# Expert stages of a mixture-of-experts trunk in fp32 blocks of 64 tokens on two column halves of TensorE

## The reference

```python
def moe(h, w_router, router_bias, w1, w3, w2):        # 16 experts, top 2 of one group
    idx, gate = route(ht, w_router, router_bias)       # T tokens -> 2 experts each
    ...                                                # slots sorted by expert, in blocks
    def expert_block(args):
        e, tok, g = args
        xb = ht[tok]                                   # rows gathered, 1024 wide
        hid = jax.nn.silu(xb @ w1[e]) * (xb @ w3[e])   # 1024 -> 512, twice
        return (hid @ w2[e]) * g[:, None]              # 512 -> 1024
    ...                                                # each token: sum of its two rows
```

## Time and profile before

| | us |
|---|---|
| three timed runs | 1637.46, 1641.4, 1643.38, median 1641.4 |
| the profiled execution | 1641.54, its span 1639.8 |
| PE busy over the span | 1403.7 (86%) |
| DVE busy | 1111.4 (68%) |
| ACT busy | 714.6 (44%) |
| bytes moved by DMA | 357.57 MB |

### The profile page before, as it was taken

How to read it: one execution, slowest core, us unless ns; L and a number is a source line. 1 busy time by engine, 2 the same in 40 slices (tenths; PEclk the granted TensorE clock), 3 DMA queues, 4 the chain that set the end, 5 groups by cost and what they waited for, 6 DMA issues and landing times. The chain is left out here.

```text
span 1639.8 us, 20695 instructions
## 1 busy us (share of the span) xinstructions
PE 1403.7 (86%) x6750; PEld 985.6 (60%) x6751; DVE 1111.4 (68%) x1475; ACT 714.6 (44%) x822; POOL 163.1 (10%) x144
## 2 busy tenths in 40 slices
PE   4788989457967899999999299799996789999990
PEld 2454555224446788888887144388653678878770
DVE  2379999974777886596553451376556788888844
ACT  3101101042345685585552330166433567777732
POOL 0000000000321010011010200000002101112201
PEclk9899999778988999999999599899997899999995
DMA  9457456308017997799564600040161799999935
GB/s 342 150 194 250 152 206 230 115 22 326 39 39 282 356 399 268 274 400 398 207 256 165 265 1 0 21 83 2 25 245 39 281 365 399 398 399 397 399 137 192
DMA packets 164095, 357.57 MB, mean 218 GB/s; under 512 B 7776, under 2 KB 35152, under 8 KB 164048
## 3 DMA queue, kind: packets, MB, share of 16 engines
q1 hardware_dynamic: 148848, 301.39, 50.3%
q0 software_dynamic: 8784, 31.99, 5.1%
q10 hardware_dynamic: 6416, 23.60, 3.6%
HBM read 318.57 MB, written 38.37 MB: 218 GB/s over the span
## 5 line engine op out<-in xcount | busy, mean ns | idle before, releaser
L717 DVE TENSOR_TENSOR W_LO<-W_RAW,W_HI 128x2048 fp32r<-128x2048 f32 x192 | 433.5, 2287 | 136.4 <-ACT W_HI L710 129.1
L710 ACT ACTIVATE W_HI<-W_RAW 128x2048 fp32r<-128x2048 f32 x192 | 363.0, 1912 | 97.8 <-DMA W_RAW<-in_moe_w 54.7
L1406 PE MATMUL PS<-W_HI,XLO 128*128 128x512 f32 x624 | 252.8, 405 | 28.3 <-DVE XLO L1541 28.2
L1408 PE MATMUL PS<-W_HI,XHI 128*128 128x512 f32 x624 | 247.7, 397 | 0.0
L1407 PE MATMUL PS<-W_LO,XHI 128*128 128x512 f32 x624 | 247.6, 397 | 0.0
L1184 PE MATMUL PS<-HT,RING 128*128 128x512 f32 (+1 forms) x512 | 174.6, 497 | 8.5 <-DVEq L1255 8.5
L1406 PEld LDWEIGHTS PS<-W_HI,XLO 128*128 128x128 f32 x624 | 120.0, 192 | 57.8 <-issue 25.9
L1184 PEld LDWEIGHTS PS<-HT,RING 128*128 128x128 f32 x512 | 97.6, 195 | 88.4 <-issue 72.7
L1408 PEld LDWEIGHTS PS<-W_HI,XHI 128*128 128x128 f32 x624 | 120.0, 192 | 26.2
L1407 PEld LDWEIGHTS PS<-W_LO,XHI 128*128 128x128 f32 x624 | 120.0, 192 | 23.7
L1406 PE MATMUL PS<-W_HI,HLO 128*128 128x512 f32 x312 | 124.8, 400 | 3.4 <-ACT YO L1497 3.4
(11 more groups left out here) (238 smaller groups left out, 1809.7 us busy)
## 6 DMA issues: line engine op xcount, KB each, us to landing
W_RAW<-in_moe_w SPq DMA_DIRECT2D x192, 1024.0 KB, 11.0
RING<-in_w_mod SPq DMA_DIRECT2D x24, 2048.0 KB, 14.3
moe_out<-YO ACTq DMA_DIRECT2D x39, 512.0 KB, 6.2
moe_out<-HT SPq DMA_DIRECT2D x20, 512.0 KB, 8.4
RING<-in_conv_pw SPq DMA_DIRECT2D x16, 512.0 KB, 5.3
ROWS<-rows_of_layer SPq DMA_DIRECT2D x12, 512.0 KB, 6.4
RING<-in_attn_w_qkv SPq DMA_DIRECT2D x3, 2048.0 KB, 8.1
moe_in<-RING SPq DMA_DIRECT2D x10, 512.0 KB, 3.0
```

What stands on the lines that cost most here:

```text
L710: nc.scalar.activation(part(W_HI[q], p), part(WRAW[q], p), ACT.Copy).then_inc((w2_hi if q == 2 else w_hi)[L], 1)
L717: nc.vector.tensor_tensor(part(W_LO[q], p), part(WRAW[q], p), part(W_HI[q], p).bitcast(F32), ALU.subtract).then_inc(lo[L], 1)
L1406: pe.matmul(to, lo, W_HI[q][:, at:at + 512], start=start, stop=False)
L1408: return pe.matmul(to, hi, W_HI[q][:, at:at + 512], start=False, stop=stop)
```

## The change

- A block is now 64 rows (`SUB`). `MAXB`, the index tables, the result tensor's rows and the router's arithmetic follow; INFO has a third row that tells in which of two places an expert's weights land (`home_of`).
- The products are plain fp32: no high and low parts, no `split_hi` and `split_lo`. In `up` the w3 product goes to output partitions 0 to 63 and the w1 product to 64 to 127 of one PSUM bank, by `tile_position`, each with the same 64 stationary columns; in `down` the two halves of the 1024 output columns do the same.
- Weights land in two places by the parity of the expert, and ACT (w1 and the first half of w2) and DVE (w3 and the second half of w2) copy them to the fixed place from which PE multiplies (`place`). The first expert's weights land there directly. A load waits for the same weight of the expert before to have landed and for the one before that to be copied away. Loads start after the first gather.
- Other buffers take the freed room: the combine's gathers and the QKV weight use other slots, and the QKV weight's third part is loaded before the last stores are waited for.

The diff of the stage, cut to its core (indentation reduced; `blocks_of`, `last_block`, `expert_of`, `cell_of` and `home_of` are register reads of INFO like `load_of`):

```diff
-MAXB = [TILES * 2 + NE, LT * 2 + NE]
 DEEP = [TILES, LT]
+SUB = P // 2
+DEEP_SUB = [2 * TILES, 2 * LT]
+MAXB = [2 * TILES * P // SUB + NE, 2 * LT * P // SUB + NE]
+MINB = [2 * TILES * P // SUB, 2 * LT * P // SUB]
+WSLOT = 4096
...
-    XHI = shared("XHI", [P, KT, P], F32R)
...
-    W1_HI = shared("W1_HI", [P, 4096], F32R)
-    W1_LO = shared("W1_LO", [P, 4096], F32R)
...
-    WRAW, W_HI, W_LO = (W1_RAW, W3_RAW, W2_RAW), (W1_HI, W3_HI, W2_HI), (W1_LO, W3_LO, W2_LO)
+    XT = shared("XT", [P, KT, SUB])
+    XG = shared("XG", [SUB, D])
+    YO = shared("YO", [P, 512])
+    SIL = shared("SIL", [SUB, FE])
+    HID = shared("HID", [SUB, FE])
+    HTT = shared("HTT", [P, FE // P, SUB])
+    WR = shared("WR", [P, 9 * WSLOT])
+W1, W3, W2 = (WR[:, n * WSLOT:(n + 1) * WSLOT] for n in (2, 3, 1))
...
-    return RING[:, (0, 3, 4)[q // 4], (q % 4) * D:(q % 4 + 1) * D]
-QKV_SLOT = (1, 5, 2)
+    return RING[:, (1, 2, 3)[q // 4], (q % 4) * D:(q % 4 + 1) * D]
+QKV_SLOT = (4, 0, 5)
...
+PART = WSLOT // 2
+def load_weight(sp, L, e, kind):
+    name, landed = {1: ("moe_w1", w1_in), 2: ("moe_w2", w2_in), 3: ("moe_w3", w3_in)}[kind]
+    if e:
+        for p in range(2):
+            sp.wait_ge(landed[p], e * 16)
+        at = {1: 4 + 2 * (e % 2), 3: 5 + 2 * (e % 2), 2: 8 * (e % 2)}[kind]
+    else:
+        at = {1: 2, 3: 3, 2: 1}[kind]
+    k = FE // P if kind == 2 else KT
+    src = a[name][L].rearrange("e (k p) f -> e p k f", p=P)[e]
     for p in range(2):
...
+        half = at * WSLOT + p * PART
+        sp.dma_start(WR[:, half:half + PART].rearrange("p (k f) -> p k f", k=k // 2),
+                     src[:, p * k // 2:(p + 1) * k // 2, :]).then_inc(landed[p], 16)
 def gather(pool, L):
     src = h2d[L][:, :] if L == 0 else h2d[L][0:SEQ, :]
     pool.indirect_dma_start(out=XG[:, :], out_offset=None, in_=src,
...
+                            in_offset=bass.IndirectOffsetOnAxis(ap=icur[0:SUB, 0:1], axis=0)
                             ).then_inc(xg_in[L], 16)
...
-        split_hi(act, L, 0, 0)
-        split_hi(act, L, 0, 1)
...
-            sp.wait_ge(xg_in[L], 32)
-            load_weights(sp, L, 1, (0, 1))
-            load_weights(sp, L, 0, (2,))
...
+            n = blocks_of(sp, L)
+            sp.wait_ge(xg_in[L], 16)
+            load_weight(sp, L, 0, 2)
+            for e in range(1, NE):
+                for kind, placed in ((1, (w1_placed,)), (3, (w3_placed,)),
+                                     (2, (w2_placed_low, w2_placed_high))):
+                    if e >= 3:
+                        for one in placed:
+                            sp.wait_ge(one[L], (e - 1) * (1 if kind == 2 else 2))
+                    load_weight(sp, L, e, kind)
             if L == 0:
...
+                sp.wait_ge(w3_placed[L], 2 * NE - 2)
                 load_qkv(sp, 2)
...
+                sp.wait_ge(w1_placed[L], 2 * NE - 2)
                 load_qkv(sp, 0)
-            rows = sp.compute_val(n * 16)
+                sp.wait_ge(w2_placed_low[L], NE - 1)
+                sp.wait_ge(w2_placed_high[L], NE - 1)
+                load_qkv(sp, 1)
+            rows = sp.compute_val(n * 32)
             sp.wait_ge(y_out[L], rows)
             load_row(sp, L, 1, 5, 5, gates_in[L])
             if L == 0:
                 load_row(sp, L, 0, 5, 4, gates_in[L])
-                load_qkv(sp, 1)
             else:
...
             def turn_x(b):
                 pe.wait_ge(xg_in[L], b * 16 + 16)
+                pe.sem_inc(rows_seen[L], 1)
                 for k in range(KT):
+                    ins = pe.transpose(PXT[k // 4][:, k % 4 * SUB:(k % 4 + 1) * SUB], XG[:, k * P:(k + 1) * P],
+                                       ident[0:SUB, 0:SUB])
                 ins.then_inc(xg_turned[L], 1)
...
-                pe.matmul(to, lo, W_HI[q][:, at:at + 512], start=start, stop=False)
-                pe.matmul(to, hi, W_LO[q][:, at:at + 512], start=False, stop=False)
-                return pe.matmul(to, hi, W_HI[q][:, at:at + 512], start=False, stop=stop)
-            def up(load, q, bank, done):
+            def turn_hid(b):
+                pe.wait_ge(hid_ready[L], b + 1)
+                pe.sem_inc(hid_seen[L], 1)
+                for k in range(FE // P):
+                    ins = pe.transpose(PHB[:, k * SUB:(k + 1) * SUB], HID[:, k * P:(k + 1) * P],
+                                       ident[0:SUB, 0:SUB])
+                ins.then_inc(hid_turned[L], 1)
+            def up(load, half_way):
                 for k in range(KT):
                     if k % 4 == 0:
...
+                        pe.wait_ge(w3_placed[L], load * 2 + (1 + k // 4))
+                        pe.wait_ge(w1_placed[L], load * 2 + (1 + k // 4))
+                    for g, w in enumerate((W3, W1)):
+                        ins = pe.matmul(PUV[g * SUB:(g + 1) * SUB, :], XT[:, k, :], w[:, k * FE:(k + 1) * FE],
+                                        start=(k == 0), stop=(k == KT - 1), tile_position=(0, g * SUB))
+                    if k == 3:
+                        half_way()
+                ins.then_inc(up_done[L], 1)
+            def down(load):
+                pe.wait_ge(w2_placed_low[L], load + 1)
                 for k in range(FE // P):
...
+                    if k == FE // P // 2:
+                        pe.wait_ge(w2_placed_high[L], load + 1)
+                    for c in range(2):
+                        at = k * D + c * 512
+                        ins = pe.matmul(PYO[c * SUB:(c + 1) * SUB, :], HTT[:, k, :], W2[:, at:at + 512],
+                                        start=(k == 0), stop=(k == FE // P - 1), tile_position=(0, c * SUB))
+                ins.then_inc(down_done[L], 1)
             turn_x(0)
+            for landed, placed in ((w1_in, w1_placed), (w3_in, w3_placed)):
+                for p in range(2):
+                    pe.wait_ge(landed[p], 16)
+                    pe.sem_inc(placed[L], 1)
+            pe.wait_ge(xTa[L], 1)
             pe.wait_ge(xTb[L], 1)
...
+            up(0, lambda: None)
             turn_x(1)
...
+            def block_step(b, before, y_taken):
+                load = expert_of(pe, b)
+                pe.wait_ge(xTa[L], b + 1)
                 pe.wait_ge(xTb[L], b + 1)
                 pe.wait_ge(hid_ready[L], b)
...
+                up(load, lambda: turn_hid(b - 1))
                 turn_x(b + 1)
...
+                pe.wait_ge(hT_ready[L], b)
+                if y_taken is not None:
+                    pe.wait_ge(ya_ready[L], y_taken)
+                else:
+                    for p, placed in enumerate((w2_placed_low, w2_placed_high)):
+                        pe.wait_ge(w2_in[p], 16)
+                        pe.sem_inc(placed[L], 1)
+                down(before)
+            block_step(1, 0, None)
             with pe.Fori(2, n) as b:
...
+                block_step(b, expert_of(pe, b - 1), b - 1)
+            last = last_block(pe, L)
             turn_hid(last)
...
+            pe.wait_ge(hT_ready[L], n)
+            pe.wait_ge(ya_ready[L], last)
+            down(expert_of(pe, last))
+        def place(eng, copy, L, load, home, kind, halves, placed):
+            at, landed = {1: (home + 4 * WSLOT, w1_in), 3: (home + 5 * WSLOT, w3_in), 2: (home * 4, w2_in)}[kind]
+            to = {1: W1, 2: W2, 3: W3}[kind]
+            for p in halves:
+                eng.wait_ge(landed[p], load * 16 + 16)
+                copy(to[:, p * PART:(p + 1) * PART], WR[:, bass.ds(at + p * PART, PART)]).then_inc(placed[L], 1)
         @block.scalar
         def _(act):
...
+            def x_low(b):
+                act.wait_ge(xg_turned[L], b + 1)
+                nc.scalar.activation(XT[:, 0:4, :], PXT[0].rearrange("p (k n) -> p k n", k=4),
+                                     ACT.Copy).then_inc(xTa[L], 1)
+            def silu(b, again_):
+                act.wait_ge(up_done[L], b + 1)
+                if again_:
+                    act.wait_ge(hid_ready[L], b)
+                nc.scalar.activation(SIL[:, :], PUV[SUB:P, :], ACT.Silu).then_inc(silu_done[L], 1)
+            def take_hid(b):
+                act.wait_ge(hid_turned[L], b + 1)
+                nc.scalar.activation(HTT[:, :, :], PHB.rearrange("p (k n) -> p k n", k=4),
+                                     ACT.Copy).then_inc(hT_ready[L], 1)
+            def y_store(b, rows, again_):
+                act.wait_ge(down_done[L], b + 1)
+                if again_:
+                    act.wait_ge(y_out[L], b * 32)
+                nc.scalar.activation(YO[:, :], PYO, ACT.Copy).then_inc(ya_ready[L], 1)
+                act.wait_ge(ya_ready[L], b + 1)
+                for c in range(2):
+                    act.dma_start(yd[L][rows, c * 512:(c + 1) * 512], YO[c * SUB:(c + 1) * SUB, :]).then_inc(
+                        y_out[L], 16)
+            def up_next(load, b):
+                after = expert_of(act, b + 1)
+                home = home_of(act, b + 1)
+                with act.If(load < after):
+                    place(act, copy, L, after, home, 1, (0, 1), w1_placed)
```

(73 more changed lines are left out.)

307 lines of the change are left out of this document (92 added, 215 removed).

## The result

The changed kernel takes 1645.4 us (median of 8 runs, 1643.3 to 1647.9) against 1641.6 of the kernel before on the same chip; the ratio is 1.0025, 95% interval 1.0014 to 1.0036. The forecast was 1628 with 0.58 on faster: the time is inside the range, the sign is wrong. The profiled execution has a span of 1644.0 us, 4.2 more than before.

The account below looks back on a forecast made before the run. PE's blocks were taken to bound layer 0's expert stage, weight bytes over DMA layer 1's. 1641.5 + 4.2 (layer 0) - 17.5 (layer 1) + 3.6 (routing) - 3.5 (combine) = 1628.3 us; range 1604 to 1663.

Parts of the forecast that it names:

- The blocks: PE's work in the expert stages: 12.1 us per 64-row block, where 17.68 bought 128 rows.
- rival 2: Transposes in a block cost by their 64 moving columns: c is 11.4 us, time 1604; 10%.
- Rival 1: Switching PE between halves and whole array costs a drain, 0.35 us each, four a block: c 13.0, time 1665; 25%.
- rival 3: Matmuls on the two column halves do not run beside one another: block 22.4 us, time 2195; 1%.
- rival 4: PE is late for gathers, register loads or ACT's chain at expert changes, 0.3 us a block: 1641, no change; 14%.
- The first weights: Start of each expert stage: loads start some 9 us earlier, and the first six megabytes take about 18.5 us.
- One-block experts: After expert 1's weights, an expert with one block costs 17.1 us of DMA at 398 GB/s, more than c.
- DMA behind PE again: Late layer 1: DMA alone would bring expert 15 at about 1539, some 7 us before PE is ready.
- The tail: End of each expert stage after the last `up`: turn, two `down`s and the wait between them, 10 us.
- The half clock after waits: After PE's idle gaps at the first experts the clock is at half: 1.7 us for one such window.
- Routing: Wider tables in front of each expert stage: 0 to 4 us a layer, taken 1.8 each, +3.6 in all.
- the stretch between the stages: From layer 0's expert stage to layer 1's: combine taken as -3.5 us, layer 1's routing as +1.8.

Follow-up runs that it names:

- Run 6: Changed kernel with each gather of 64 rows done as 128 half rows into 128 partitions, and 4 transposes of 128 columns: 1631.7 us (ratio 0.9940).
- run 9: Changed kernel with each weight's rows dealt out in 8 KB pieces, PE's transposes reading every fourth column: 1661.7 us (ratio 1.0128).
- run 12: Changed kernel with reordered tail, early expert 1 weights, gather into 128 partitions, 8 KB weight pieces and columns dealt out by existing DVE operations: 1595.9 us (ratio 0.9728).
- run 1: Changed kernel with the weights of experts 3 to 15 fetched for only 8 of 128 partitions: 1600.7 us (ratio 0.975 to the kernel before).
- Run 3: Changed kernel with only the last block's order changed, ACT taking the last hidden rows before issuing the previous block's stores: 1632.9 us (ratio 0.9944).

## Why the prediction was wrong, by its own steps

Profiled against profiled, -13.2 was forecast and +4.2 came: 17.4 us. What each step contributed (c is PE's time for one block; layer 0 and 1 in turn):

- **The blocks.** c was 12.1 and is 11.63, and 11.75 with changes: the 316.5 us stretch was forecast as 329.1 (-12.6), the 17 blocks of layer 1 as 208.7 against 199.9 (-8.8, without the waits at experts 11 and 12). The transposes with 64 moving columns cost less than 0.109 each, as rival 2 has it. How the rest divides was not separated: if they hold PE for all of their 1.03 us, four changes between halves and whole array cost 10.60 - 10.31 = 0.29 us; if they go wholly by their columns (0.65, rival 2's figure), the changes cost 11.63 - 10.31 - 0.65 = 0.67, where 0.47 was taken. Rival 1, with 1.4, falls either way; so do rival 3 (the pairs run beside one another) and rival 4 (PE is busy 316.48 of 316.50 us). The Trainium skill ("TensorEngine Tiling (Array Packing)", Key Properties) has such a change drain the engine; the trace agrees only with a drain of 0.07 to 0.17 us, an estimate from these two sums.
- **The first weights.** Forecast: six megabytes in 18.5 us, from 314 GB/s and 399. They took 22.7 in layer 0, sharing DMA with the gathers (340 GB/s); how much is theirs was not separated. Expert 1's SiLU is some 5.4 and 4.3 us later than forecast, counted from each stage's first turn.
- **One-block experts, the step that failed.** 17.1 us was bytes over 398 GB/s, and 398 came from slices in which PE's blocks of 128 rows were gathered into 128 partitions. Measured: 18.4 us in layer 0 and 18.6 in layer 1, +3.7 and +6.0. Run 6 names the cause: with the gather alone changed, DMA is back from 376 to 395 GB/s and the step in layer 1 at 17.1 (18.0 in layer 0). I took the highest rate seen for a mix of transfers the change itself altered. Packets of 2 KB, which my expectation for run 9 blamed, were in that mix already; pieces of 8 KB lift the rate beyond it, to 419 (run 12).
- **DMA behind PE again.** "DMA alone would bring expert 15 some 7 us before PE is ready": the prediction looked at the last expert only. DMA is late at experts 11 and 12, +12.5 us (16.3 + 19.8 - 2 x 11.8), at the end of a row of experts with one block each (8 to 11): PE takes such an expert in 11.85 us, DMA in 18.6. The rate is the smaller part of it: run 6, with 395 GB/s, still takes 16.3 and 17.2 us there, 9.8 too many. What the cheaper blocks saved in layer 1 (8.8) was not there to be had; without the transfers this stretch is 12.0 us shorter (run 1).
- **The tail.** Ten microseconds a layer were put down without a working; 14.6 and 15.7 came, +10.3. The queue on ACT was in the diff: in the loop `take_hid` stands behind a store, which PE's next `up` hides, and at the end nothing does. Run 3 gives it back.
- The half clock after waits (1.7 a layer, forecast apart) is contained in the steps above: -3.4. Routing (+1.6 for +1.8), the stretch between the stages (-1.5 for -1.7) and the last combine (-0.1 for 0) came as forecast.

The sum: -12.6 - 8.8 + 9.7 + 9.7 + 12.5 + 10.3 - 3.4 = 17.4. PE's share was priced too high and DMA's too low; that the time stayed in the range is luck, because they nearly cancel. The sign is lost by 4.2 us, and each of the four positive terms is larger than that: no one of them alone decides it. The price of a block, which the prediction calls the term that decides, was off by 4% and in the good direction; what decided was when transfers arrive, and an ACT queue.

## What to carry to other kernels

Before a step of compute is made cheaper, take the transfers away: a run without them shows how much of the gain waits on them (here 35 us of gain without the weights of experts 3 to 15, 4 us of loss with them). A rate of DMA belongs to a mix of transfers; when a change halves the partitions that a gather lands in, or the rows that it takes, the old rate is no longer evidence. And read the last turn of a loop by itself: what the next iteration hides in the middle stands open at the end.

## What the runs showed of the hardware

Three things I had not expected. A gather of 64 rows into 64 partitions slows the transfers beside it: over the time that its packets take, the weights' queue moves 368 GB/s (32.06 MB / 0.918 / 95 us), and 382 when the same bytes land in 128 partitions, as in the kernel before. A packet's time has a fixed part: the medians in the weights' queue are 88 ns for 2 KB and 162 for 4 KB in the changed kernel and 313 for 8 KB in run 9, about 13 ns plus 0.0366 ns a byte; so 16 engines give 372, 404 and 419 GB/s. The Trainium skill ("DMA: Bandwidth & Descriptors", Why small descriptors are slow) states a fixed cost of some 3 cycles a packet, beside one cycle for each 32 bytes. The sign agrees; by the fit, 32 bytes take 1.17 ns and the fixed part is worth some 11 of them, an estimate. And a strided read is not free on either engine: fp32 transposes of every fourth column take 1.17 us for 8 in place of 0.71, DVE's product of two inputs read every fourth column 1089 ns in place of 683.
